# Hybrid attention and mixture-of-experts step: the last expert tile's rows added by one-hot products, the first gather ahead of three constant loads, one changed order on VectorE

## What is computed

```python
h = ln_plain(x) * (1 + sc2) + sh2
y = hier_moe(h, ...)          # 16 experts, each token goes to 2 of them
x = ln_affine(DEEPNORM_ALPHA * x + g2 * y, ln2_g, ln2_b)

# hier_moe, for each expert e:
gg, uu = split(t @ w_gate_up[e])                       # 1024 -> 2 x 512
out += combine[:, e:e+1] * ((silu(gg) * uu) @ w_down[e])   # 512 -> 1024
```

## Time and profile before

| what | value |
|---|---|
| median of 3 runs | 1366.25 us (1364.53 to 1366.25) |
| the profiled execution | 1362.08 us |
| its span (first to last instruction) | 1360.2 us |
| mean granted TensorE clock | 0.956 of 2.4 GHz |
| PE busy | 1237.8 us (91%) |
| DVE busy | 954.8 us (70%) |
| ACT busy | 658.1 us (48%) |
| DMA | 301.05 MB, mean 221 GB/s |

### The profile page before, as it was taken

How to read it: one execution, slowest core, us unless ns; L and a number is a source line. 1 busy time by engine, 2 the same in 40 slices (tenths; PEclk the granted TensorE clock), 3 DMA queues, 4 the chain that set the end, 5 groups by cost and what they waited for, 6 DMA issues and landing times.

```text
span 1360.2 us, 20484 instructions
## 1 busy us (share of the span) xinstructions
PE 1237.8 (91%) x6683; PEld 997.9 (73%) x6683; DVE 954.8 (70%) x1718; ACT 658.1 (48%) x1050; POOL 209.7 (15%) x312
## 2 busy tenths in 40 slices
PE   7999999999999899998998999993899999999940
PEld 4777777777888788887876788773688888888830
DVE  5765531839461688888777526688799999999937
ACT  1522222223222677776763213123487787788822
POOL 0023221020232000011111001001212111112101
PEclk9999999999999999999999999995799999999985
DMA  9977664462646778642004533457899999999935
GB/s 349 294 243 240 209 224 171 155 224 83 214 140 174 179 210 214 189 130 84 25 23 136 191 110 139 150 193 274 298 327 365 373 381 391 391 383 381 337 116 141
DMA packets 150338, 301.05 MB, mean 221 GB/s; under 512 B 20380, under 2 KB 31196, under 8 KB 150264
## 3 DMA queue, kind: packets, MB, share of 16 engines
q1 hardware_dynamic: 122424, 232.72, 50.0%
q0 software_dynamic: 21920, 62.13, 14.6%
q10 hardware_dynamic: 5920, 5.24, 1.3%
HBM read 258.71 MB, written 53.38 MB: 229 GB/s over the span
## 4 chain that ended last, share of the span: by engine, by line
PE 79%; DVE 10%; DMA 5%; issue 2%; ACT 2%; SPq 1%; POOL 0%; DVEq 0%; ACTq 0%; POOLq 0%
PE psum_pair L1751 9%; PE psum_pair L1753 8%; PE psum_pair L1752 8%; PE psum_pair L1853 6%; PE psum_pair L2037 5%; PE psum_pair L2039 5%; PE psum_pair L2038 5%; PE psum_pair L1920 4%; PE psum_pair L1922 3%; PE psum_pair L1921 3%; PE psum_pair L1864 3%; PE psum_pair L1879 3%; PE psum_pair L2052 3%; PE psum_pair L2053 3%; PE psum_pair L2054 3%
## 5 line engine op out<-in xcount | busy, mean ns | idle before, releaser
L1751 PE MATMUL psum_pair<-w_parts,h_hi 128*128 128x512 f32 x520 | 207.2, 398 | 3.0 <-DVE h_lo L1277 3.0
L1753 PE MATMUL psum_pair<-w_parts,h_lo 128*128 128x512 f32 x520 | 203.5, 391 | 0.0
L1752 PE MATMUL psum_pair<-w_parts,h_hi 128*128 128x512 f32 x520 | 203.2, 391 | 0.0
L1127 DVE TENSOR_TENSOR w_parts<-w_raw,w_parts 128x1024 fp32r<-128x1024 f32 x72 | 83.3, 1221 | 92.9 <-ACT w_parts L845 92.3
L985 ACT ACTIVATE p_unnormed<-psum_pair,minus_max 128x640 f32<-128x640 f32 (+1 forms) x160 | 113.4, 711 | 67.6 <-DVE minus_max L1355 66.3
L1853 PE MATMUL psum_pair<-k_bundle,q_bundle 128*128 128x512 f32 (+1 forms) x576 | 122.9, 341 | 13.8 <-ACT p_unnormed L985 10.1
L1355 DVE TENSOR_REDUCE minus_max<-psum_pair 128x1 f32<-128x640 f32 (+1 forms) x160 | 111.8, 715 | 30.6 <-PE psum_pair L1853 28.2
L1751 PEld LDWEIGHTS psum_pair<-w_parts,h_hi 128*128 128x128 f32 x520 | 98.0, 189 | 30.9 <-issue 11.6
L1753 PEld LDWEIGHTS psum_pair<-w_parts,h_lo 128*128 128x128 f32 x520 | 97.9, 188 | 21.0
L1853 PEld LDWEIGHTS psum_pair<-k_bundle,q_bundle 128*128 128x128 f32 x576 | 88.1, 193 | 34.2 <-issue 21.2
L1752 PEld LDWEIGHTS psum_pair<-w_parts,h_hi 128*128 128x128 f32 x520 | 98.2, 189 | 19.4
(11 more groups left out here) (347 smaller groups left out, 2567.9 us busy)
## 6 DMA issues: line engine op xcount, KB each, us to landing
w_raw<-in_w_gate_up SPq DMA_DIRECT2D x76, 512.0 KB, 8.2
w_raw_c<-in_w_gate_up SPq DMA_DIRECT2D x72, 512.0 KB, 8.8
w_raw_b<-in_w_down SPq DMA_DIRECT2D x72, 512.0 KB, 7.9
w_raw<-in_w_in SPq DMA_DIRECT2D x52, 512.0 KB, 9.0
ada_raw<-in_w_ada SPq DMA_DIRECT2D x32, 512.0 KB, 7.7
k_bundle<-k_transposed SPq DMA_DIRECT2D x28, 384.0 KB, 8.3
q_transposed<-turned_staging POOLq DMA_DIRECT2D x40, 256.0 KB, 6.3
ada_raw_early<-in_w_ada SPq DMA_DIRECT2D x16, 512.0 KB, 8.9
```

The costliest lines, as they stand in the source:

```text
L1127: dve.tensor_tensor(w_parts[b % 2][:, 1, c], w_raw[:, c], w_parts[b % 2][:, 0, c].bitcast(F32), ALU.subtract).then_inc(lo_done, 1)
L1751: pe.matmul(out, a_hi, hi, start=kk == 0, stop=False)
L1752: pe.matmul(out, a_hi, lo, start=False, stop=False)
L1753: return pe.matmul(out, a_lo, hi, start=False, stop=kk == KD - 1)
```

## The change

Three edits:

1. **DVE's order.** In the first tiles chunk 1 of tile 0's gate moves ahead of `rest_x(0)`, and `times_up(0, 1)` and `rest_x(1)` move ahead of the four chunks of tile 1's up block.
2. **First gather.** POOL issues the gather for tile 0 ahead of the three constant loads.
3. **Last tile.** The last tile's output no longer goes through DRAM. Its pair rows in `pair_scr` are set to zero by one scatter of a zeroed `xs`, while tile `middle` is under way. `moe_over` is given when the scatter of tile `middle` has landed. ACT writes the last tile's weighted output as `yo_hi`, DVE its remainder `yo_lo`; DVE builds from the token numbers of the tile's slots a one-hot matrix `last_pick` for each token tile; and for each token tile PE adds into one PSUM pair the identity times `ya`, the identity times `yc` (both f32), and `last_pick` times `yo_hi` and `yo_lo` (both f32r). `combine` reads that sum from PSUM, so `ya + yc` on DVE is gone. The buffers `yc`, `yo_hi`, `yo_lo`, `ya` and `last_pick` now lie over `w_parts0` and `w_parts1`.

```diff
@@ ACT, after the loop
+            act.wait_ge(xs_in, 16 * (middle + 3))
+            act.activation(xs[:].rearrange("p (k q) -> p k q", q=P), over(ones[:], 1, [P, KD, P]), ACT.Copy, scale=0.0).then_inc(xs_clear, 1)
             split_hi_moe(down_block(middle))
...
-            take_out(middle + 1, last_block(middle + 1)[0])
+            act.wait_ge(moe_used, used(last_block(middle + 1)[0] + 1))
+            act.wait_ge(y_free, middle + 1 + OFF)
+            act.activation(yo_hi[:], pair[3][:], ACT.Copy, scale=out_now[:, 2:3].bitcast(F32)).then_inc(y_copied, 1)
@@ DVE, first tiles
-            split_lo_moe((0, 0, 0), (0,))
+            split_lo_moe((0, 0, 0), (0, 1))
             rest_x(0)
-            split_lo_moe((0, 0, 0), range(1, NC_CH))
+            split_lo_moe((0, 0, 0), (2, 3))
...
             silu(0)
-            split_lo_moe(up_block(1))
             times_up(0, 1)
             rest_x(1)
+            split_lo_moe(up_block(1))
             rest_hidden(0)
@@ DVE, tail
+            dve.wait_ge(y_free, middle + 1 + OFF)
+            for tt in range(NT):
+                link(dve.tensor_scalar(token[:, tt:tt + 1], out_now[:, 1:2], -float(tt * P), None, ALU.add))
+            link(dve.tensor_tensor(last_pick[:], over(places[:], 1, [P, NT, P]),
+                                   over(token[:], 2, [P, NT, P]), ALU.is_equal))
+            dve.wait_ge(y_copied, middle + 2 + OFF)
+            dve.scalar_tensor_tensor(yo_lo[:], pair[3][:], out_now[:, 2:3].bitcast(F32), yo_hi[:].bitcast(F32),
+                                     ALU.mult, ALU.subtract).then_inc(al_done, 1)
...
-                dve.wait_ge(y_in[tt], 32)
-                link(dve.tensor_tensor(y, y, yc[:, tt], ALU.add))
-                link(dve.tensor_tensor(y, y, g2[:, cnd], ALU.mult))
+                dve.wait_ge(sums_ready, tt + 1)
+                link(dve.tensor_tensor(y, pair[tt % 4][:], g2[:, cnd], ALU.mult))
@@ PE, tail
+            for tt in range(NT):
+                pe.wait_ge(y_in[tt], 32)
+                if tt == 4:
+                    pe.wait_ge(z_done, 1)
+                if tt == 3:
+                    pe.wait_ge(al_done, middle + 3 + OFF)
+                for h in range(2):
+                    cols = slice(h * CW, (h + 1) * CW)
+                    pe.matmul(pair[tt % 4][:, cols], ident[:], ya[:, tt, cols], start=True, stop=False)
+                    pe.matmul(pair[tt % 4][:, cols], ident[:], yc[:, tt, cols], start=False, stop=False)
+                if tt == 0:
+                    pe.wait_ge(al_done, middle + 3 + OFF)
+                for h in range(2):
+                    cols = slice(h * CW, (h + 1) * CW)
+                    pe.matmul(pair[tt % 4][:, cols], last_pick[:, tt], yo_hi[:, cols], start=False, stop=False)
+                    last = pe.matmul(pair[tt % 4][:, cols], last_pick[:, tt], yo_lo[:, cols], start=False, stop=True)
+                last.then_inc(sums_ready, 1)
@@ POOL
-            pool.dma_start(ln2_g, t["ln2_g"][0:1, :].to_broadcast([P, D])).then_inc(s7_in, 16)
-            for c in range(2):
-                pool.dma_start(g2[:, c], mod_scr[c:c + 1, 5 * D:6 * D].to_broadcast([P, D])).then_inc(s7_in, 16)
...
             gather(row_now[:])
+            pool.dma_start(ln2_g, t["ln2_g"][0:1, :].to_broadcast([P, D])).then_inc(s7_in, 16)
+            for c in range(2):
+                pool.dma_start(g2[:, c], mod_scr[c:c + 1, 5 * D:6 * D].to_broadcast([P, D])).then_inc(s7_in, 16)
...
+                if left == 1:
+                    pool.tensor_copy(row_now[:], table[:, bass.ds(tile + 1, 1), 0]).then_inc(row_set, 1)
+                    pool.wait_ge(row_set, tile + 1)
+                    pool.nop().then_inc(pool_turn, 1)
+                    pool.wait_ge(xs_clear, 2)
+                    pool.indirect_dma_start(out=pair_scr, out_offset=bass.IndirectOffsetOnAxis(ap=row_now[:, 0:1], axis=0), in_=xs[:],
+                                            in_offset=None, bounds_check=last_pair, oob_is_err=False).then_inc(zeroed, 16)
...
                 pool.wait_ge(y_st, 16 * (tile + 1))
+                if left == 1:
+                    pool.wait_ge(zeroed, 16)
+                    pool.nop().then_inc(moe_over, 1)
...
-            store_rows(middle + 1, 0)
```

34 lines of the change are left out of this document (20 added, 14 removed).

## The result

The changed kernel takes 1350.33 us (median of 4 runs, 1347.56 to 1353.6), against 1366.25 of the kernel before in the same set (4 runs): ratio 0.9884, 95% interval 0.986 to 0.9907. Run twice more in later sets it came to 0.9864 (0.9849 to 0.988) and 0.9862 (0.9839 to 0.9885). The forecast of 1347.8 us is a ratio of 0.9865. The profiled execution took 1349.8 us with a span of 1348.0, against 1362.08 and 1360.2 before.

A forecast was written before the change was run, and what follows sets the result against it. PE was taken to bound the expert loop, with DVE close behind, so gains lie at its ends: 8.5 us at the start plus 9.9 in the tail, 18.4 off the median 1366.25, gives 1347.8 us; range 1345 to 1350.

The forecast's parts named there:

- The sum of 18.4 us: Whole kernel: 8.5 us won by the start of the loop plus 9.9 us in the tail.
- First gather, 3.0 us: Expert stage start: gather issued ahead of the constants lands in 6.9 us, so PE starts tile 0 3.0 us earlier.
- Rival A: Expert stage start: x loads on SP's queue still slow the gather, so 3.0 us go, giving 1350.9; chance 0.18.
- DVE's order, 3.0 us: Tile 0 to tile 1: the new order on DVE brings gate of tile 1 forward by 3.0 us more.
- The clock, 2.58 us: Gate of tile 1: PE's gap shrinks to about 1.8 us, the clock does not fall, and 2.58 us come back.
- rival C: Tail: pair rows come after 1313.6, PE's clock is at 1.2 GHz, total 1367.4, no change; chance 0.07.
- rival B: Gap ahead of gate of tile 1: clock falls anyway, 2.6 us go, giving 1350.4; chance 0.10.
- The loop keeps it: Expert loop: displaced DVE differences fit with 1.3 us left, costing nothing; 18.0 us per tile, no PE wait.
- The tail, 9.9 us: After the last weight product: the last tile's new way through PE ends the kernel 9.9 us earlier, before the start's shift.
- The end, held constant at 6.36: Kernel's end: from the start of `finish_z(4)` to the end of the span stays 6.36 us.

The follow-up runs named there:

- one_chunk: Changed kernel with DVE's `rest_x(0)` behind one difference of gate weights instead of two; 1344.34 us, ratio 0.9859 to the kernel before.
- after_again: The changed kernel run a second time, unaltered, in a later set on another chip; 1345.97 us, ratio 0.9864 to the kernel before.
- after_third: The changed kernel run a third time, unaltered, in the set on TensorE's clock; 1345.73 us, ratio 0.9862 to the kernel before.
- after: The changed kernel in its first set, with the first profile; 1350.33 us, ratio 0.9884 to the kernel before.
- The parts alone: Kernel before with only the moved gather and DVE's new order, ratio 0.9959; changed kernel with those two edits undone, ratio 0.9949.
- start_only: Kernel before with the gather ahead of the constants and DVE's new order, old tail kept; 1360.08 us, ratio 0.9959.
- pool_bias: Changed kernel with GpSimd adding the bias for sample tiles 2 and 3 and plain stores replacing accumulating ones; 1350.27 us, ratio 0.9901.

## Why the prediction was right

The sum of 18.4 us was measured as 15.8 (0.9884), 18.6 and 18.9 (0.9864 and 0.9862 of 1366.25). Its steps one by one:

- **First gather, 3.0 us: right.** T0 is 2.9 less. The landing was sized at 6.9 us from the loop's median and took 5.3 to 5.5; as the text said, a landing sooner than 949.8 gives nothing, since DVE's two differences are the second bound. `one_chunk` shows that this bound is real and worth 0.66 us. Rival A fell: with SP's loads under way in all, the gather took 9.8 us behind the three loads of constants and 5.3 without them. The Trainium skill's rule that fed it (page "DMA: Bandwidth & Descriptors", section "Issuing engines are not separate DMA queues") says that transfers of all issuing engines share the 16 DMA engines and interleave. The trace agrees with that, since SP's `x_rows_c` also came down from 11.7 to 6.8 us; what was wrong was only to take from it that a gather without the constants ahead of it would gain nothing.
- **DVE's order, 3.0 us: right in size, short in the first profile.** From tile 0 to gate of tile 1 it took 17.70 us there, 2.1 less than before, since the clock rose late: products up to 962.09 stood 0.43 us apart, and the 48 took 14.1 us and not my 13.3. In the two later profiles of the same kernel the stage took 16.5 and 16.4, 3.3 and 3.4 less than before.
- **The clock, 2.58 us: the step that was wrong in its reason.** I read one gap of 2.15 us without a fall and took it for a rule. I also put the fall behind 1310.5 at 1313.6; a mean of 0.58 over the window from 1313 to 1314 means that it came at 1313.2, so rival C had 1.2 us of margin and not 1.6. Behind gaps of 2.00 to 2.18 us ahead of gate 1, the clock fell in 6 of 10 profiles; behind those of 2.07 to 2.15 ahead of the last `down`, in 7 of 13. By these counts rival B, at a chance of 0.10, should have had about one half. Its price was too high: from gate of tile 1 to `turn_x(2)` it is 12.8 us with the fall (`after_again`, `after_third`) and 11.2 without (after, `one_chunk`), 1.6 us. In the first profile the whole 2.4 came, by luck; in the two others 0.8.
- **The loop keeps it: right.** No wait of PE in the loop, 18.0 us per tile.
- **The tail, 9.9 us: 10.25 by X2 to F.** f32 products take 0.86 and not 0.9, token tiles 4.37 and not 4.53, DVE's 3.92. The identity products started 1.4 us behind the last weight product where the clock had not fallen, as said.
- **The end, held constant at 6.36: wrong by 1.2 to 3.4 us.** I moved `finish_z(4)` up and left the store behind it as it was, without asking what else ends the kernel. DVE's quicker tiles push the prompt's store from 6.1 to 4.8 us behind POOL's last accumulating one (1355.15 less 1349.09, and 1339.60 less 1334.80). POOL's store did not move up by those 1.26 us, and the span closes 3.9 to 4.0 us behind its landing. Where the two overlap more, both are longer: the prompt's 3.5 to 5.7 us in place of 2.6, POOL's up to 9.2 in place of 7.2.

So the mechanisms at the two ends of the loop were right, and the total was right partly by luck. By the stages of the profiles the change is worth 14.3, 14.7 and 16.2 us (after, `after_again`, `after_third`) and not 18.4: the start gives 7.1 to 7.4 in place of 8.5, and the tail 10.3 less the 1.2 to 3.4 given back. By the medians it is worth 15.8 to 18.9. The profiled execution of before is 4.2 us quicker than its median, that of after 0.5, and no profile shows what makes the difference.

**What stays open.** The parts alone, by their ratios, are worth 5.6 and 7.0 us, 12.6 together; the whole is worth 15.8 to 18.9. By their profiles they are worth 8.9 and 9.1, 18.0 together, and the whole 14.3 to 16.2. In both parts the profiled execution was the quickest of its set (1352.24 of 12 runs with a median of 1360.08; 1352.87 of 6 with 1359.24). Over the 12 runs of `start_only` the mean granted clock goes from 0.963 in the quickest to 0.953 in the slowest, so the slow ones spend longer at 1.2 GHz somewhere; where, a profile of one of them would have to show, and there is none. Nothing in the profiles points to the part ahead of the change: its first product stands at 940.3 in the mean of the four with the old tail and at 941.3 in the ten with the new.

## What to carry to other kernels

When a stage ends sooner, follow every path to the end of the program, not only the one of the last instruction: ask which transfers of other queues are still under way at the new time, and whether they moved up as well, since the gain can be given back there and no engine's busy time shows it. Speeding up one engine is worth only the distance to the next thing due, here the second gather: full clock in tile 0 saved PE 1.5 us and the start of the next tile 0.5. And one gap that passed without a fall of the clock is one throw of a coin; look at the same gap in several executions before pricing it.

## What the runs showed of the hardware

- The granted clock behind an idle gap of about 2 us of PE did not go by the gap's length here: it fell behind one of 2.00 us and stayed up behind one of 2.18. Each fall came 0.3 to 1.6 us after PE had resumed and cost 7 or 8 products of 128 x 512 at 0.43 us in place of 0.23. Behind 1.52 us it did not fall (one profile).
- Of the last two accumulating stores of 512 KB from GpSimd, issued 1.0 us apart, the first lands in 5.2 to 5.7 us and the second in 6.9 to 9.2, with a DMA share of 1.03 at 175 GB/s (before, 1349.5 to 1355.0); plain ones in their place take 2.9 us (`pool_bias`). A plain store of 512 KB from SP takes 2.6 us alone and 3.5 to 5.7 issued 4.8 us behind the second of those two.
- A VectorE instruction of 128 x 1024 with two inputs in SBUF took 3.33 and 3.06 us in place of 1.23 and 1.28 while GpSimd added two SBUF tiles of 128 x 1024 (`pool_bias`).
- An f32 product of 512 columns takes 0.86 us back to back at 2.4 GHz, less than the 0.95 of the earlier trace rows.
